# Half tiles of the expert stage: new load order, second side dealt from the far end, scatter-add in two parts

## The chip, the cores and the metric

The kernel runs on one core of one Trainium2 chip. The time is the device time of one launch in microseconds (us). Names used below: PE is TensorE, ACT is ScalarE, DVE is VectorE, POOL is GpSimd, SP is SyncE, whose only work here is to issue DMAs. PEclk is the granted TensorE clock, where 1.00 is 2.4 GHz and 0.50 is 1.2 GHz.

## The reference, cut to what matters

One decoder layer over 2048 prompt tokens and 64 sample tokens (D = 1024). The change touches only its last part, a mixture of experts: every token goes to 2 of 16 experts (both in the same group of four), each expert is a SwiGLU with weights of 1024 x 256 (gate), 1024 x 256 (up) and 256 x 1024 (down), all float32, and the two results are added per token:

```
eid = g_idx[:, None] * EXPERTS_PER_GROUP + top_i
hg = jnp.einsum('td,edf->tef', xt, w_gate)
hu = jnp.einsum('td,edf->tef', xt, w_up)
act = jax.nn.silu(hg) * hu * gates[..., None]
return jnp.einsum('tef,efd->td', act, w_down).reshape(shp)
```

After it comes a norm over each token's sum, a gain, and the addition of the residual x2.

## The kernel before

The expert stage (`moe`) sorts the 4224 pairs of token and expert by expert and cuts them into 42 tiles of 128 rows. The first 32 (`NWHOLE`) are whole: all rows belong to one expert, the weights are split in high and low parts, and a tile takes PE some 9.3 us. The last 10 (`NPAIR`, "steps" 0 to 9 below) hold the remainders: each has two halves, or sides, of 64 rows (`HROWS`), with an expert of its own. There is room for 20 halves (`NHALF`), numbered in the order of the experts; how many exist depends on the routing. Half h sits at step h on side 0 for h below 10, and at step h - 10 on side 1 otherwise. The pair of loads of a half that does not exist is issued with a condition that is false (`cond`, from `plan_h`), so it moves nothing.

For a step PE does, in this order: gate and up of tile t (`gate_up_halves`, L3150, 32 matmuls), the transpose of the tokens of tile t+2 (L3139), down of tile t-1 (`down_halves`, L3164, 16 matmuls), and the transpose of the activations (L3102). ACT copies the down result out of PSUM into one of two buffers `o` (L2732), and POOL adds it to the rows of `acc` in DRAM by an indirect DMA with addition (`store`, L2664). A token can occur in two tiles, so a store waits until the one before it has landed. ACT waits, before it fills a buffer of `o`, until the store two tiles back has landed. POOL's queue between two stores holds the routing weights of a later tile (`weigh`, L2653 to L2655) and the gather of the tokens of a later tile (`refill`, L2658).

SP issues the weight loads in program order: `half_gate_up` (L2564, two loads of 1 MB) and `half_down` (L2575, one of 1 MB). Rings of buffers: gate and up 5 deep on side 0 and 2 on side 1, down 3 and 2 (`GU_RING`, `D_RING`). A load waits until the tile that used its buffer is done; a wait of SP holds everything behind it. The order before is gate/up of (step, side) = (0,0), (0,1), (1,1), (1,0), (2,0), (3,0), (4,0), then down of (0,0), (0,1), (1,1), (1,0), (2,0), then per step the refills of the rings. In steps 5, 6, 7 and 8 SP also loads 5, 4, 4 and 4 tiles of the residual x2 (L2547, 0.5 MB each), behind that step's gate/up refill.

When all stores have landed, SP loads the 17 tiles of `acc` (L2620) and the other engines finish the output.

The slot of a pair is computed on DVE (L2906 to L2911, tiny instructions in a chain in which each waits for the one before), the row addresses of the scatter are `to` (L2941), one column for each tile.

Of the kernel before, what the change touches and what calls it, by code (L numbers as in the profile page):

```python
# [17 lines left out]
U32 = mybir.dt.uint32  # L18
ALU = mybir.AluOpType
# [3 lines left out]
P = 128  # L23
# [49 lines left out]
class Stage:  # L73
# [17 lines left out]
    def sem(self, name):  # L91
        return self.top.get(f"{self.tag}_{name}")
# [2267 lines left out]
HROWS = P // 2  # L2360
# [36 lines left out]
def moe(nc, T, top, lg, plan_in):  # L2397

    E16 = [P, NT, NE]
    with Stage(nc, top, "ex") as s:  # L2400
# [19 lines left out]
        et, plan = s.sb("et", [1, 4, NWHOLE]), s.sb("plan", [1, 3, NWHOLE], I32)  # L2420
        eh, plan_h = s.sb("eh", [1, 3, NHALF]), s.sb("plan_h", [1, 2, NHALF], I32)
# [38 lines left out]
        names = ("halved G2_in G2_samples eps_set warm tailed hit tiled tiled_late numbered tail_out weighed wt_ready to_ready summed rooted rstd gained gain_moved y_pool g_ready y_ready y_out cleared5 consts5 w5_in mm5 mod5 row5 out5 ident_in step de exped hot counted planned matched turned rows_ready x_flipped x_moved_a x_moved_v w_rounded w_split d_rounded d_split a_split gu_done th_ready "  # L2460
# [25 lines left out]
        yv = T["o_y_prompt"].rearrange("a (n p) d -> p (a n) d", p=P)  # L2486
        rows_of = lambda t: slice(0, NS) if t == LAST else slice(0, P)
# [11 lines left out]
        def _(sp):  # L2499
# [49 lines left out]
            def half_expert(step, side, always):  # L2549
                h = step + side * NPAIR  # L2550
                e = sp.value_load(plan_h[0:1, 0, h:h + 1], min_val=0, max_val=NE - 1)
                return e, {} if always else {"cond": sp.value_load(plan_h[0:1, 1, h:h + 1], min_val=0, max_val=1)}
# [40 lines left out]
            half_gate_up(2, 0)  # L2593
            half_gate_up(3, 0)
            half_gate_up(4, 0)
            half_down(0, 0)
            half_down(0, 1)
            half_down(1, 1)
            for step in range(NPAIR):
                if step == 0:  # L2600
                    half_down(1, 0)
                    half_down(2, 0)
                for side in (1, 0):
                    if step + GU_RING[side] < NPAIR:
# [20 lines left out]
            sp.wait_ge(S["st_even"], (HT + 1) * 16)  # L2625
            sp.wait_ge(S["st_odd"], (HT + 1) * 16)
# [8 lines left out]
        def _(pool):  # L2635
# [24 lines left out]
            def store(t):  # L2660
                pool.wait_ge(S["o_out_a"], t * 2 + 4)
                if t:
                    pool.wait_ge(sem("st", (t - 1) % 2), ((t - 1) // 2 + 2) * 16)
                pool.indirect_dma_start(T["acc"], bass.IndirectOffsetOnAxis(to[:, t:t + 1], 0), o[:, t % 2, :], None, compute_op=ALU.add).then_inc(sem("st", t % 2), 16)  # L2664
# [17 lines left out]
            pool.wait_ge(S["st_even"], (HT + 1) * 16)  # L2682
            pool.wait_ge(S["st_odd"], (HT + 1) * 16)
# [6 lines left out]
        def _(act):  # L2690
# [37 lines left out]
            def out(t, par, q):  # L2728
                act.wait_ge(S["d_done"], t + NSL + 1)
                act.wait_ge(sem("st", par), q * 16 + 16)  # L2730
                for c in range(2):
                    A(o[:, par, c * 512:(c + 1) * 512], ps_o[:, c * 512:(c + 1) * 512], ACT.Copy).then_inc(S["o_out_a"], 1)  # L2732
# [28 lines left out]
            def step(t, k, i, more=True):  # L2761
                par = k % 2
                gate(t, par)
                if more:
                    move_x(t + 2, par)
                    slot = weights_of(t + 2, (k + 2) % U, i + (k + 2) // U)
                    round_w(t + 2, par, range(PARTS // 2), slot)
                out(t - 1, 1 - par, i * (U // 2) + (k - 1) // 2)
# [15 lines left out]
            for t in range(NWHOLE - 2, NTILE):  # L2784
# [3 lines left out]
                out(t - 1, (t - 1) % 2, (t - 1) // 2)  # L2788
# [6 lines left out]
            out(NTILE - 1, 1, HT - 1)  # L2795
# [30 lines left out]
        def _(dve):  # L2826
# [425 lines left out]
```

## Time and profile before

| | us |
|---|---|
| median of 3 runs | 1485.31 (1484.14 to 1490.89) |
| profiled execution, its own time | 1483.67 |
| its span, first to last instruction | 1481.9 |
| last matmul of the last whole tile, to the last store landed | 1270.4 to 1432.7 |

Busy shares of the span: PE 87%, DVE 69%, ACT 48%, POOL 40%. All times in the rows are us from the start of the span. The page cuts the span into 40 equal slices of 37 us; a digit is the busy share in tenths. The stage of the half tiles lies in slices 35 to 39. In the rows of DMA queues, q1 carries the loads that SP issues, q0 those of POOL (gathers and scatter-adds); the share is that of the time of the core's 16 DMA engines, and the two together may come out a little over 1.

### The profile page before, as it was taken

The numbers are of one execution on the slowest core, as the hardware profiler recorded it, in microseconds if no ns is written. First come the engines' busy times: TensorE is split into PE (matmuls) and PEld (weight loads), VectorE is DVE, ScalarE is ACT, GpSimd is POOL, SyncE is SP. The second block draws the span as 40 slices with busy tenths as digits, with TensorE's granted clock in tenths as the row PEclk, the third lists the DMA queues.
The fourth block names the chain that finished last, engine by engine and source line by source line (L and its number), as shares of the span: only waits on it lengthen the run. The fifth ranks groups of instructions, "written<-read, shape, count | busy, mean of one in ns | idle before, by whom it ended". The sixth has DMA issues, their size and how long they took to land. (4 is left out here: it accounts for less than half of the span.)

```text
span 1481.9 us, 23003 instructions
## 1 busy us (share of the span) xinstructions
PE 1281.9 (87%) x6972; PEld 951.6 (64%) x6972; DVE 1017.3 (69%) x1914; ACT 708.9 (48%) x1551; POOL 596.2 (40%) x730
## 2 busy tenths in 40 slices
PE   4999999969998999699999996289999999669930
PEld 1688888846675666588888884178888888323310
DVE  3788888827676778566667764999999999200026
ACT  2432333213345768334444432268898998212234
POOL 1107766832223880022222330346565755212115
PEclk9999999979998999899999997599999999889975
DMA  9423444479897653335444446658999898999989
GB/s 328 147 88 128 164 168 179 167 232 335 297 298 181 188 175 121 127 110 166 161 145 142 142 138 231 220 173 228 299 314 278 245 281 239 315 337 342 330 254 365
DMA packets 163031, 325.30 MB, mean 220 GB/s; under 512 B 23140, under 2 KB 103141, under 8 KB 160590
## 3 DMA queue, kind: packets, MB, share of 16 engines
q1 hardware_dynamic: 136854, 251.88, 49.4%
q0 software_dynamic: 19072, 54.83, 14.8%
q10 hardware_dynamic: 7024, 17.60, 3.2%
q8 instruction: 40, 0.66, 0.2%
q14 instruction: 41, 0.34, 0.1%
HBM read 314.63 MB, written 97.73 MB: 278 GB/s over the span
## 5 line engine op out<-in xcount | busy, mean ns | idle before, releaser
L2664 POOL DMA_INDIRECT scratch_acc<-route_o,ex_to x42 | 80.6, 1918 | 235.1 <-ACT route_o L2732 138.1
L2929 DVE TENSOR_TENSOR ex_w_lo<-route_wgu,ex_w_hi 128x1024 fp32r<-128x1024 f32 x128 | 150.5, 1216 | 2.9 <-issue 1.9
L147 PE MATMUL fr_ps_m<-fr_whi,fr_hl 128*128 128x512 f32 (+1 forms) x384 | 138.8, 361 | 0.9 <-DVE fr_wlo L658 0.5
L149 PE MATMUL fr_ps_m<-fr_whi,fr_hl 128*128 128x512 f32 (+1 forms) x384 | 136.2, 355 | 0.0
L148 PE MATMUL fr_ps_m<-fr_wlo,fr_hl 128*128 128x512 f32 (+1 forms) x384 | 136.0, 354 | 0.0
L2035 POOL TENSOR_SCALAR mx_st<-mx_st 128x1 f32<-128x1 f32 x68 | 38.1, 561 | 228.9 <-ACT mx_j L2083 127.8
L2705 ACT ACTIVATE ex_w_hi<-route_wgu 128x1024 fp32r (+1 forms) x128 | 128.6, 1064 | 1.9 <-issue 1.9
L147 PE MATMUL mx_ps_m<-mw_area,mx_hT 128*128 128x512 f32 x272 | 108.8, 400 | 4.1 <-issue 2.1
L2999 DVE SCALAR_TENSOR_TENSOR ex_gates<-ex_gates,ex_ps_h 128x256 f32<-128x256 f32 x42 | 17.4, 414 | 133.6 <-ACT ex_gates L2713 133.2
L148 PE MATMUL mx_ps_m<-mw_area,mx_hT 128*128 128x512 f32 x272 | 107.2, 394 | 0.0
L149 PE MATMUL mx_ps_m<-mw_area,mx_h_lo 128*128 128x512 f32 x272 | 107.1, 394 | 0.0
L147 PE MATMUL ex_ps_h<-ex_w_hi,ex_xT 128*128 128x512 f32 x256 | 103.6, 405 | 0.1
L148 PE MATMUL ex_ps_h<-ex_w_lo,ex_xT 128*128 128x512 f32 x256 | 100.9, 394 | 0.0
L3150 PE MATMUL ex_ps_h<-route_wgu,ex_xT_whole 128*64 128x512 f32 x192 | 73.1, 622 | 14.2 <-DMA route_wgu<-in_w_exp_up_dram 14.2
L2653 POOL TENSOR_SCALAR ex_eq<-ex_x,route_rc 128x2 f32<-128x2 f32 x42 | 83.4, 1985 | 0.1
L147 PEld LDWEIGHTS fr_ps_m<-fr_whi,fr_hl 128*128 128x128 f32 x384 | 72.5, 189 | 15.0 <-issue 3.0
L451 ACT ACTIVATE fr_io<-fr_ps_m,fr_st 128x512 f32<-128x512 f32 (+1 forms) x45 | 27.4, 617 | 113.2 <-PE fr_ps_m L149 113.1
L148 PEld LDWEIGHTS fr_ps_m<-fr_wlo,fr_hl 128*128 128x128 f32 x384 | 72.6, 189 | 10.4
L149 PEld LDWEIGHTS fr_ps_m<-fr_whi,fr_hl 128*128 128x128 f32 x384 | 72.6, 189 | 10.3
L2969 DVE TENSOR_TENSOR ex_wd_lo<-route_wd,ex_wd_hi 128x1024 fp32r<-128x1024 f32 x64 | 76.2, 1231 | 3.2 <-ACT ex_wd_hi L2723 3.0
L1609 ACT ACTIVATE at_sc<-at_sc,at_nm 128x256 f32<-128x256 f32 (+1 forms) x128 | 62.7, 492 | 18.3 <-DVE at_nm L1689 18.2
L2732 ACT ACTIVATE route_o<-ex_ps_o 128x512 f32<-128x512 f32 x84 | 45.4, 595 | 47.1 <-PE ex_ps_o L3164 42.0
(544 smaller groups left out, 3562.0 us busy)
## 6 DMA issues: line engine op xcount, KB each, us to landing
route_wd<-in_w_exp_down_dram SPq DMA_DIRECT2D x46, 1024.0 KB, 10.0
route_wgu<-in_w_exp_gate_dram SPq DMA_DIRECT2D x44, 1024.0 KB, 12.8
route_wgu<-in_w_exp_up_dram SPq DMA_DIRECT2D x44, 1024.0 KB, 15.2
scratch_rec<-fr_w SPq DMA_DIRECT2D x16, 1112.0 KB, 4.2
s_rec<-scratch_rec SPq DMA_DIRECT2D x32, 556.0 KB, 6.3
scratch_proj<-fr_io SPq DMA_DIRECT2D x16, 640.0 KB
scratch_acc<-in_zeros_dram SPq DMA_DIRECT2D x18, 512.0 KB, 5.6
fr_w<-in_w_ada_dram SPq DMA_DIRECT2D x8, 1024.0 KB, 9.6
```

Of the source, the lines that this page charges most:

```text
L147: nc.tensor.matmul(out, hi, w_hi, start=first, stop=False)
L148: nc.tensor.matmul(out, hi, w_lo, start=False, stop=False)
L149: return nc.tensor.matmul(out, lo, w_hi, start=False, stop=final)
L1609: last = A(sc[:, p % 2, h, k0:], sc[:, p % 2, h, k0:], ACT.Exp, scale=-1.0, bias=nm[:, p % 2, h:h + 1], accum_out=sm[:, p % 2, h:h + 1])
L2035: last = nc.gpsimd.tensor_scalar(a[:, col + m:col + m + 1], a[:, col + m:col + m + 1], c, EPS, ALU.mult, ALU.add)
L2653: chain.then(nc.gpsimd.tensor_scalar(eq2[:, :], x[:, n, D + 2:], C["place"][:, t:t + 1], None, ALU.is_equal))
L2664: pool.indirect_dma_start(T["acc"], bass.IndirectOffsetOnAxis(to[:, t:t + 1], 0), o[:, t % 2, :], None, compute_op=ALU.add).then_inc(sem(" ...
L2705: A(w_hi[:, par, c * PW:(c + 1) * PW], wgu[:, bass.ds(slot * (KD * 2 * DE) + c * PW, PW)], ACT.Copy).then_inc(S["w_rounded"], 1)
L2732: A(o[:, par, c * 512:(c + 1) * 512], ps_o[:, c * 512:(c + 1) * 512], ACT.Copy).then_inc(S["o_out_a"], 1)
L2929: vec.tensor_tensor(w_lo[:, par, c * PW:(c + 1) * PW], wgu[:, bass.ds(slot * (KD * 2 * DE) + c * PW, PW)], w_hi[:, par, c * PW:(c + 1) * P ...
L2969: vec.tensor_tensor(wd_lo[:, k, :], wd[:, bass.ds(slot * (2 * D) + k * D, D)], wd_hi[:, k, :].bitcast(F32), ALU.subtract).then_inc(S["d_sp ...
L3150: last = nc.tensor.matmul(ps_h[rows, t % 2, :], xT_whole[t % 2][:, k, rows], gu_of(step, side)[:, k, :], start=(k == 0), stop=(k == KD - 1))
```

## The change

1. The half on side 1 of step s is now number 19 - s instead of 10 + s. On DVE this takes five small instructions where three were.
2. SP's order: the first down loads (0,0), (0,1), (1,1) come before gate/up (2,0); then down (1,0), gate/up (3,0), down (2,0), gate/up (4,0).
3. The store of each of the ten half tiles is two indirect DMAs of 64 rows, one per side. The second waits until the first has landed, and the next tile's store waits for the second. For the second, the addresses of rows 64 to 127 are copied to partitions 0 to 63 (`to_lower`), by one small DMA that POOL issues before its first store. All 64 rows of a side are transferred, whether the half exists or not (the addresses of rows without a token point behind the tokens' rows). `stored(t)` gives the value of the semaphore at which tile t has landed; the waits are rewritten with it.

```
@@ half_expert
-                h = step + side * NPAIR
+                h = NHALF - 1 - step if side else step
@@ sync
             half_gate_up(1, 1)
             half_gate_up(1, 0)
-            half_gate_up(2, 0)
-            half_gate_up(3, 0)
-            half_gate_up(4, 0)
             half_down(0, 0)
             half_down(0, 1)
             half_down(1, 1)
+            half_gate_up(2, 0)
             for step in range(NPAIR):
                 if step == 0:
                     half_down(1, 0)
+                    half_gate_up(3, 0)
                     half_down(2, 0)
+                    half_gate_up(4, 0)
@@ store
-                    pool.wait_ge(sem("st", (t - 1) % 2), ((t - 1) // 2 + 2) * 16)
-                pool.indirect_dma_start(T["acc"], bass.IndirectOffsetOnAxis(to[:, t:t + 1], 0), o[:, t % 2, :], None, compute_op=ALU.add).then_inc(sem("st", t % 2), 16)
+                    pool.wait_ge(sem("st", (t - 1) % 2), stored(t - 1))
+                if t < NWHOLE:
+                    pool.indirect_dma_start(T["acc"], bass.IndirectOffsetOnAxis(to[:, t:t + 1], 0), o[:, t % 2, :], None, compute_op=ALU.add).then_inc(sem("st", t % 2), 16)
+                    return
+                for side in range(2):
+                    h = slice(side * HROWS, (side + 1) * HROWS)
+                    if side:
+                        pool.wait_ge(S["lower_in"], 16)
+                        pool.wait_ge(sem("st", t % 2), stored(t) - 16)
+                    pool.indirect_dma_start(T["acc"], bass.IndirectOffsetOnAxis(to_lower[:, t - NWHOLE:t - NWHOLE + 1] if side else to[h, t:t + 1], 0), o[h, t % 2, :], None, compute_op=ALU.add).then_inc(sem("st", t % 2), 16)
@@ gpsimd
             pool.wait_ge(S["to_ready"], 1)
+            pool.dma_start(to_lower[:, :], to[HROWS:P, NWHOLE:]).then_inc(S["lower_in"], 16)
@@ vector
-            ts(side, half_no, NPAIR - 0.5, 1.0 - NHALF, ALU.is_ge, ALU.mult)
-            tt(half_no, half_no, side, ALU.add)
-            chain.then(vec.scalar_tensor_tensor(sf, half_no, float(HROWS), sf, ALU.mult, ALU.add))
+            ts(side, half_no, NPAIR - 0.5, None, ALU.is_ge, ALU.bypass)
+            chain.mark(vec.scalar_tensor_tensor(sf, half_no, float(HROWS), sf, ALU.mult, ALU.add))
+            ts(half_no, half_no, -4.0 * HROWS, (2.0 * NHALF - 1) * HROWS, ALU.mult, ALU.add)
+            tt(side, side, half_no, ALU.mult)
+            tt(sf, sf, side, ALU.add)
```

## Rows read from the trace of the kernel before

**Rows 1.** Page, the 40 slices: PE, DMA share, GB/s.
```profile
PE   4999999969998999699999996289999999669930
DMA  9423444479897653335444446658999898999989
GB/s 328 147 88 128 164 168 179 167 232 335 297 298 181 188 175 121 127 110 166 161 145 142 142 138 231 220 173 228 299 314 278 245 281 239 315 337 342 330 254 365
```
**Rows 2.** Waits, 1255 to 1435: who <- for whom: us in total, times, longest.
```profile
POOL scratch_acc L2664 <- DMA scratch_acc<-route_o,ex_to: 22.4, 4, 9.4
PE ex_ps_h L3150 <- DMA route_wgu<-in_w_exp_up_dram: 14.2, 1, 14.2
PE ex_ps_o L3164 <- DMA route_wd<-in_w_exp_down_dram: 11.9, 1, 11.9
```
**Rows 3.** Timeline of SP's DMA issues: start, us, what.
```profile
1259.52 0.64 SPq L2564 DMA_DIRECT2D route_wgu<-in_w_exp_gate_dram  x1
...
1262.34 1.56 SPq L2564 DMA_DIRECT2D route_wgu<-in_w_exp_gate_dram  x1
1264.00 7.39 SPq L2564 DMA_DIRECT2D route_wgu<-in_w_exp_up_dram  x1
1272.83 0.17 SPq L2564 DMA_DIRECT2D route_wgu<-in_w_exp_gate_dram  x1
...
1301.39 7.62 SPq L2575 DMA_DIRECT2D route_wd<-in_w_exp_down_dram  x3
```
**Rows 4.** Timeline: DVE's last split of down weights, PE's first gate/up of halves.
```profile
1272.66 2.36 DVE L2969 TENSOR_TENSOR ex_wd_lo<-route_wd,ex_wd_hi 128x1024 fp32r<-128x1024 f32 x2 [0.62 <-ACT ex_wd_hi L2723]
...
1284.60 9.38 PE L3150 MATMUL ex_ps_h<-route_wgu,ex_xT_whole 128*64 128x512 f32 x32 [14.20 <-DMA route_wgu<-in_w_exp_up_dram]
```
**Rows 5.** The chain that ended last, in order of time: start, us, what.
```profile
1318.08 6.27 PE ex_ps_o L3164 x16
...
1324.71 7.02 PE ex_ps_h L3150 x32
1331.73 1.08 PE ex_ps_t L3139 x8
1332.82 3.58 PE ex_ps_o L3164 x16
...
1407.91 7.02 PE ex_ps_h L3150 x32
1414.92 3.46 PE ex_ps_o L3164 x16
1418.40 1.09 ACT route_o L2732 x2
...
1419.82 6.29 DMA scratch_acc<-route_o,ex_to
1426.15 0.50 issue
1426.86 5.80 DMA scratch_acc<-route_o,ex_to
```
**Rows 6.** DMA view, 1262 to 1416: queue, packets, MB, share of 16 engines.
```profile
q1 hardware_dynamic: 28098, 43.02, 80.3%
q0 software_dynamic: 2491, 9.10, 24.0%
```
**Rows 7.** Stretches: us, busy of PE, PEld, DVE, ACT, POOL, PEclk, DMA share, GB/s.
```profile
1295.00:1300.00 5.00, 5.00 (x25) 3.03 (x25) 0.37 (x1) 2.45 (x5) 0.76 (x1) 1.00 1.10 350
...
1310.00:1315.00 5.00, 0.00 (x0) 0.00 (x0) 0.00 (x0) 0.00 (x0) 0.00 (x0) 0.50 1.05 410
...
1415.00:1420.00 5.00, 3.91 (x20) 1.25 (x18) 0.90 (x2) 1.72 (x4) 0.18 (x1) 1.00 0.64 151
```
**Rows 8.** Timeline of POOL: two stores in a row [idle before <- releaser].
```profile
1398.18 1.58 POOL L2664 DMA_INDIRECT scratch_acc<-route_o,ex_to  x1 [9.47 <-ACT route_o L2732]
...
1410.09 1.59 POOL L2664 DMA_INDIRECT scratch_acc<-route_o,ex_to  x1 [9.43 <-DMA scratch_acc<-route_o,ex_to]
```
**Rows 9.** DMA view, 1426.9 to 1432.7: engines' busy tenths in 40 slices.
```profile
DMA  0000000000000099037696959599999999820000
```
**Rows 10.** Timeline: DVE's slot arithmetic, then POOL's issue of a small DMA.
```profile
943.88 0.19 DVE L2830 TENSOR_TENSOR ex_stau<-ex_stau,ex_srow 128x34 f32<-128x34 f32 x1
944.11 0.22 DVE L2911 SCALAR_TENSOR_TENSOR ex_tail<-ex_stau,ex_tail 128x34 f32<-128x34 f32 x1
...
927.87 0.53 POOL L2643 DMA_DIRECT2D ex_row<-in_b_ada_dram  x1 [0.29 <-POOL ex_row L2639]
```

More of the change, by code:

```diff
@@ L2420, in moe @@
         et, plan = s.sb("et", [1, 4, NWHOLE]), s.sb("plan", [1, 3, NWHOLE], I32)
+        to_lower = s.sb("to_lower", [HROWS, NPAIR], U32)
         eh, plan_h = s.sb("eh", [1, 3, NHALF]), s.sb("plan_h", [1, 2, NHALF], I32)
@@ L2459, in moe @@
         junk = wd[:, 3 * D:4 * D]
-        names = ("halved G2_in G2_samples eps_set warm tailed hit tiled tiled_late numbered tail_out weighed wt_ready to_ready summed rooted rstd gained gain_moved y_pool g_ready y_ready y_out cleared5 consts5 w5_in mm5 mod5 row5 out5 ident_in step de exped hot counted planned matched turned rows_ready x_flipped x_moved_a x_moved_v w_rounded w_split d_rounded d_split a_split gu_done th_ready "
+        names = ("lower_in halved G2_in G2_samples eps_set warm tailed hit tiled tiled_late numbered tail_out weighed wt_ready to_ready summed rooted rstd gained gain_moved y_pool g_ready y_ready y_out cleared5 consts5 w5_in mm5 mod5 row5 out5 ident_in step de exped hot counted planned matched turned rows_ready x_flipped x_moved_a x_moved_v w_rounded w_split d_rounded d_split a_split gu_done th_ready "
                  "sg_ready a_ready a_flipped a_moved d_done o_out_a st_even st_odd").split()
@@ L2486, in moe @@
         yv = T["o_y_prompt"].rearrange("a (n p) d -> p (a n) d", p=P)
+        stored = lambda t: (t // 2 + 2 + max(0, (t - NWHOLE) // 2 + 1)) * 16
         rows_of = lambda t: slice(0, NS) if t == LAST else slice(0, P)
@@ L2624, in _ @@
             sp.dma_start(G2[:, 0, :], mod_row(T, 5)).then_inc(S["G2_in"], 16)
-            sp.wait_ge(S["st_even"], (HT + 1) * 16)
-            sp.wait_ge(S["st_odd"], (HT + 1) * 16)
+            sp.wait_ge(S["st_even"], stored(NTILE - 2))
+            sp.wait_ge(S["st_odd"], stored(NTILE - 1))
             for t in range(NT):
@@ L2681, in _ @@
                 store(t)
-            pool.wait_ge(S["st_even"], (HT + 1) * 16)
-            pool.wait_ge(S["st_odd"], (HT + 1) * 16)
+            pool.wait_ge(S["st_even"], stored(NTILE - 2))
+            pool.wait_ge(S["st_odd"], stored(NTILE - 1))
             for n, t in enumerate(BY_POOL):
@@ L2726, in slot_of, with out @@
                 return act.value_load(plan[0:1, 2, bass.ds(t, 1)], min_val=0, max_val=NSL - 1)
-            def out(t, par, q):
+            def out(t, par, landed):
                 act.wait_ge(S["d_done"], t + NSL + 1)
-                act.wait_ge(sem("st", par), q * 16 + 16)
+                act.wait_ge(sem("st", par), landed)
                 for c in range(2):
@@ L2767, in step @@
                     round_w(t + 2, par, range(PARTS // 2), slot)
-                out(t - 1, 1 - par, i * (U // 2) + (k - 1) // 2)
+                out(t - 1, 1 - par, (i * (U // 2) + (k - 1) // 2) * 16 + 16)
                 move_a(t)
@@ L2787, in _ @@
                     move_x_whole(t + 2)
-                out(t - 1, (t - 1) % 2, (t - 1) // 2)
+                out(t - 1, (t - 1) % 2, stored(t - 3))
                 if t < NWHOLE:
@@ L2794, in _ @@
                     A(aT[:, :, :], ps_a[:, 0:2 * P].rearrange("p (k n) -> p k n", k=2), ACT.Copy, scale=0.5).then_inc(S["a_moved"], 1)
-            out(NTILE - 1, 1, HT - 1)
+            out(NTILE - 1, 1, stored(NTILE - 3))
             act.wait_ge(S["eps_set"], 1)
```

## Prediction

> **What bounds the kernel now.** The slices of the page come first: PE is near full almost everywhere, and in the stage of the half tiles (slices 35 to 38) it drops while the DMA share stands at 9 [rows 1]. The waits of that stretch name what PE waits for: once 14.2 us for the gate/up weights of step 0, once 11.9 us for the down weights of step 0 [rows 2]. SP's timeline tells why. Gate/up (0,0) is issued at 1259.52, (0,1) at 1262.34, and then come 6 MB of gate/up for steps 2 to 4 before the first down load at 1301.39 [rows 3]. The same timeline tells how many halves exist: a load that moves data takes SP 0.6 us or far more once the queue is full, one whose condition is false 0.17 us. (0,1) is real, (1,1) at 1272.83 is not, nor is any later load of side 1. So there are 11 halves: ten on side 0, one on side 1. The bytes agree: 11 halves of 3.15 MB and 16.5 tiles of x2 of 0.524 MB are 43.3 MB, and q1 moved 43.02 MB from 1262 to 1416 [rows 6].
>
> The same rows hold what decides. Over those 154 us the two queues take 80.3% + 24.0%, more than all of the DMA engines' time. They are full from the first half's load until the last x2 tile, and only after 1415 does the share fall (0.64) [rows 6, 7]. PE's two stalls are thus a matter of order, but the stretch as a whole is also bound by DMA. From step 1 on, PE runs at 7.02 + 1.08 + 3.58 + 0.37 = 12.06 us a step [rows 5]. At the end, two stores follow each other: from 1419.82 to 1432.7 [rows 5].
>
> **The change part by part.**
>
> *The first steps.* Half number 19 doesn't exist, so (0,1) moves nothing, and gate/up (0,0) alone has to land before step 0. In the trace both together, 4.2 MB, let PE start at 1284.6 [rows 4]; without 2.1 MB, at the 350 GB/s of gate/up loads [rows 7], that is 6 us earlier. Two of q0's DMAs then also fall behind the data instead of ahead of it; q0's 2491 packets are 17 DMAs of 144, 24.0% of 154 us is 37 us, so 2.1 us each [rows 6]. That gives 1284.6 - 6 - 4.2 = 1274.4. PE could start at 1284.6 - 14.2 = 1270.4, so the stall becomes some 4 us. Down (0,0) can be issued from 1275.0, when DVE has split the last whole tile [rows 4], and lands long before PE wants it at about 1293: the 11.9 us go. With them goes the slow clock: 9.38 us for 7.02 at step 0 and 6.27 for 3.58 at the first down, both right after PE had stood idle and the granted clock was 0.50 [rows 4, 5, 7]. From step 0's gate/up to its down the trace has 1318.08 - 1284.60 = 33.5 us, without the 11.9 and the cold clock's 2.4 it is 19.2, so PE reaches the down of step 0 at 1293.6 instead of 1318.1, and runs it warm: 27 us are gained at this point. If DMA could follow, this would be the gain.
>
> *The moved half.* Half number 10 now sits at step 9, side 1: the 2.1 MB of gate/up (9,1) and the 1.05 MB of down (9,1). SP issues them in step 7, behind the x2 tiles of steps 5 and 6 and the down loads of steps 7 to 9. No byte is taken away, so the full stretch is as long as before, and (9,1) stands near its end. Behind gate/up (9,1) come only the x2 tiles of steps 7 and 8 (7.5 x 0.524 = 3.9 MB) and down (9,1) (1.05 MB): 5 MB, which at the 410 GB/s of loads with rows of 4 KB [rows 7] take 12.1 us. Gate/up (9,1) lands at 1416 - 12.1 = 1404, with half a microsecond for the signal 1404.5. PE, free for step 2's gate/up at 1297.5 and at 12.06 us a step, would want it at about 1381, so it stalls for some 23 us: the stall of the start has moved to the end. Step 9 starts 3.4 us before its time in the trace (1407.91) [rows 5], and a cold clock takes 2.4 us of it back. From there the path is the old one: 1.0 us gained. Bounds: 1401 if the queue wastes nothing, 1406 if the new order leaves gaps in the queue (down (1,0) makes SP wait for the last whole tile). I find none, because gate/up (1,0) and (2,0) are still queued then.
>
> *The order of loads* alone costs nothing beyond that: each load is still ahead of its use while the rings fill (gate/up (3,0) and (4,0) closest, about 1 us).
>
> *The split store, idle DMA.* The last two stores of 128 rows take 6.29 and 5.80 us with 0.50 and some more between them [rows 5]. In the last one, 14 of the 40 slices of 0.145 us pass before the first packet and 22 with packets: 2.1 us, 3.2 us, and 0.5 us for the rest [rows 9]. 64 rows halve the middle: 2.1 + 1.6 + 0.5 = 4.2 us, and with the issue between two DMAs 4.9. If the issue (1.58 us) halves too it is 4.1; the trace has no such store. Bounds for one: 2.9 and 5.8. I take 4.5. Four in a row make 18.0 us where two took 12.9: 5.1 us later.
>
> *The split store, full DMA.* The store at 1398.18 held the next one up until 1410.09: 11.9 us [rows 8], against 6.5 with the engines idle, so 5.4 us more under load. A half bears between half of that (2.7, if it grows with the rows) and all of it. This gives 7.2 to 9.9 us a half, 14.4 to 19.8 a pair. I take 7.75 and 15.5, nearer to the lower end because the rows queue behind the loads one by one. That is more than PE's 12.06, so POOL falls behind by 3.4 us a step. ACT's wait for the buffer two tiles back hides this for six or seven steps, and `weigh` and the gather, which stand behind the second half on POOL, are wanted two tiles later. First store of a half tile at 1298 (1293.6 + 3.6 + 1.1 of ACT); that of step 7 starts at 1298 + 7 x 15.5 = 1406.5 and ends, its second half with the queue easing, at 1420.3. Step 8's result leaves ACT at 1404.5 + 9.4 + 3.5 + 1.1 = 1418.5, so the lag adds 1.8 us. Then 18.0: the last store lands at 1438.3, against 1432.7: 5.6 us later. The stretch after it keeps its 49 us.
>
> *Small things.* Two more chained DVE instructions of 0.19 to 0.22 us [rows 10], on the way to the first gather: 0.4 us. The copy of `to_lower`: 0.5 us on POOL's queue [rows 10], ahead of `weigh`, which PE isn't waiting for: 0.1. Together 0.5.
>
> Sum: 5.6 + 0.5 = 6.1 us. The profiled execution of 1483.67 (span 1481.9 and 1.8 around it) becomes 1489.8; the median lies 1.6 above that execution, so 1485.3 + 6.1 = **1491.4**.
>
> The Trainium skill (DMA: Bandwidth & Descriptors, the section on the anatomy of a SWDGE DMA) gives 2.0 us plus bytes at 436 GB/s for one of POOL's DMAs. By it a store of 128 rows is an estimated 3.2 us and one of 64 rows 2.6, so that a pair costs 2 us more at any load and the tail 4. The trace has 5.8 to 11.9 us for 128 rows, so the page's figure is low for a DMA that adds; what it says for this change is that the fixed part is most of it, which speaks for the forecast at the end and against POOL falling behind.
>
> **The rivals.**
>
> *A, the halves are cheap:* a store costs in proportion to its rows, 2.9 us and 0.7 between them, loaded 6. Then a pair takes 12 us under load, POOL keeps up, and the tail is 4 x 3.6 = 14.4 for 12.9. 1.5 + 0.5 - 1.0 = +1.0: 1486.3. Against it: a third of the store at the end passes before its first packet [rows 9].
>
> *B, POOL's chain becomes the bound (slower):* each half carries all of the load's 5.4 us, 19.8 us a pair. POOL is behind by 7.7 us a step, from step 4 on ACT waits for its buffer and PE for ACT. The load eases only at about 1416, after six steps (1298 + 6 x 19.8), and the last four pairs take 9 each: 1453, 20 us late: 1505.8. It decides from 16.5 us a pair on. For it: the wait before the first packet is a fixed part.
>
> *C, DMA has room (faster):* the share above 1 contains waiting, and with loads in the order of use the engines finish the same bytes sooner. Then (9,1) lands near 1385, the stall is some 7 us, PE ends 20 us early, and the pairs are those of an idle queue: 4.5 x 2 a step, never behind. -19 + 5.1 + 0.5 = -13: 1472. Against it: the 43 MB and the stores filled 154 us without a gap [rows 6], and loads ran at the same 350 and 410 GB/s when PE stood [rows 7].
>
> *D, the deal does not do what it says:* if half 19 were loaded at step 0 the first stall would stay and only the down stall go. Eleven halves by two counts make this unlikely; it would give about 1495.
>
> **How the numbers follow.** Forecast (2 to 10 us late) 0.53, A 0.13, B 0.19, C 0.13, D 0.02. About 0.5%, 7.4 us, is what a measurement of this kernel can tell from no change. Slower by more: all of B and D and the upper 0.2 of the forecast, 0.41. Faster by more: most of C, 0.12. Within: 0.47. Range: from A's lower side, with C left out, 1480, to short of B's end, 1504.
>
> **What would show it.** In the changed profile PE's waits should read a few us for gate/up at step 0, none for down, and one of 20 us or more for gate/up at step 9; the DMA share from 1262 to about 1415 stays at 1; q1 carries the same 43 MB. Stores of 64 rows under load start 7 to 8 us apart and 4 to 5 at the end, and the last lands near 1438. If PE does not stall at step 9, the ledger of DMA time is wrong; if PE or ACT wait for stores before step 8, it is B.

## The result, and the profile after

| | before | after |
|---|---|---|
| median | 1485.31 us | 1510.85 us (1506.99 to 1512.86, 3 runs) |
| ratio | | 1.0165, 95% interval 1.0142 to 1.0188 |
| profiled execution | 1483.67 | 1512.86 |
| its span | 1481.9 | 1511.1 |
| first gather of the stage | 956.07 | 962.60 |
| PE free for half tiles | 1270.40 | 1281.38 |
| last store landed | 1432.7 | 1461.1 |

The change makes the kernel 25.5 us slower. 6.1 were forecast, and the range ended at 1504: the prediction named the right direction, was wrong in size and missed its range.

The two spans differ by 29.2 us. The last three rows of the table cut that up. 6.5 lie ahead of the first gather; 0.35 of them are the two more DVE instructions, and the rest is in code that is the same in both kernels. Over all builds below, this point falls anywhere between 954.5 and 962.8, and the kernel before by itself took 1480.2 to 1493.1 us in 17 runs on one chip, so it is put down to chance here. 4.5 lie between the first gather and PE free for half tiles (314.3 before, 318.8 after). 17.4 lie in the stage of the half tiles, counted from PE free to the last store landed (162.3 before, 179.7 after), and 0.8 behind it. Below, "the stage" is that last-but-one stretch; it doesn't contain the chance shift of the first one. Of these the forecast had 0.4 of the first and 5.6 of the third; it had nothing for the second.

The page after, the same lines as [rows 1]:

```profile
PE   5999999969998999799999993499999999799700
...
DMA  9424444489897562344444438649999898999759
```

PE's hole in slices 35 and 36 (6 and 6 before) is half filled, with 7 and 9. A new one stands in slices 38 and 39 (7 and 0 for 9 and 3), where the DMA share falls to 7 and 5: neither is the bound there. The waits of 1255 to 1465, as [rows 2], say more (columns: who <- for whom: us in total, times, longest):

```profile
POOL scratch_acc L2674 <- DMA scratch_acc<-route_o,ex_to: 56.4, 9, 8.1
ACT route_o L2743 <- DMA scratch_acc<-route_o,ex_to_lower: 40.6, 5, 12.1
...
DVE ex_gates L3015 <- POOL ex_wt L2657: 17.9, 4, 6.9
POOL scratch_acc L2674 <- DMA scratch_acc<-route_o,ex_to_lower: 17.8, 4, 5.5
...
PE ex_ps_h L3163 <- DMA route_wgu<-in_w_exp_up_dram: 8.1, 1, 8.1
...
PE ex_ps_h L3163 <- issue: 4.1, 1, 4.1
```

The 14.2 and 11.9 of PE are gone, as forecast; 4.1 is what is left at step 0 (forecast: 4). But PE waits 8.1 us once more for gate/up, not at step 9 but at step 2, and ACT, which waited for no store before, waits 40.6 us for second parts (`ex_to_lower`).

What PE waits for at step 2 is in SP's timeline (start, us, what):

```profile
1272.85 0.17 SPq L2566 DMA_DIRECT2D route_wgu<-in_w_exp_gate_dram  x1
...
1300.14 5.93 SPq L2566 DMA_DIRECT2D ex_spare<-in_w_exp_up_dram  x1
1306.83 3.89 SPq L2577 DMA_DIRECT2D ex_wd_spare<-in_w_exp_down_dram  x1
1311.50 0.55 SPq L2566 DMA_DIRECT2D ex_spare<-in_w_exp_gate_dram  x1
1312.15 4.42 SPq L2566 DMA_DIRECT2D ex_spare<-in_w_exp_up_dram  x1
1317.98 0.18 SPq L2566 DMA_DIRECT2D route_wgu<-in_w_exp_gate_dram  x1
1318.26 0.16 SPq L2566 DMA_DIRECT2D route_wgu<-in_w_exp_up_dram  x1
```

The first row is (0,1): 0.17 us, so it moves nothing, and the deal does what it says. The last two are gate/up (2,1), a half that doesn't exist either. They move nothing, yet PE waits for their signal, and SP reaches them only after gate/up (3,0), down (2,0) and gate/up (4,0), each of which holds SP for 4 to 6 us while the DMA share is 1.0 or more (an issue of 1 MB takes 0.6 us when DMA has room). PE's timeline:

```profile
1306.40 3.65 PE L3177 MATMUL ex_ps_o<-route_wd,ex_aT 128*64 128x512 f32 x16
...
1318.53 1.09 PE L3163 MATMUL ex_ps_h<-ex_spare,ex_xT_whole 128*64 128x512 f32 x1 [8.11 <-DMA route_wgu<-in_w_exp_up_dram]
```

PE starts 0.11 us after SP is through with (2,1). The chain that ended last, as [rows 5], goes through this point and is then almost nothing but stores:

```profile
1318.53 9.33 PE ex_ps_h L3163 x32
1327.86 1.09 PE ex_ps_t L3152 x8
1328.95 3.61 PE ex_ps_o L3177 x16
1332.58 1.09 ACT route_o L2743 x2
1333.68 0.27 issue
1333.95 7.28 DMA scratch_acc<-route_o,ex_to
1341.26 0.71 issue
1341.97 7.63 DMA scratch_acc<-route_o,ex_to_lower
1349.65 0.71 issue
1350.36 7.47 DMA scratch_acc<-route_o,ex_to
...
1429.13 4.62 DMA scratch_acc<-route_o,ex_to
1433.80 0.71 issue
1434.51 4.42 DMA scratch_acc<-route_o,ex_to_lower
...
1456.46 4.65 DMA scratch_acc<-route_o,ex_to_lower
```

The gate/up matmuls of step 2 take 9.33 us and not 7.02: behind PE's wait the granted clock is 0.50 until 1323 ("cold clock" below), then 0.99. From 1333.95 on each part waits for the one before. Before, the same stretch was PE's 12.06 us a step [rows 5]; now it is POOL's pairs.

### The profile page after: what moved, and what is told of

Same layout as the page of the kernel before. It is cut to its first block and busy times, and to the rows that moved or that the text cites. A ratio compares the mean times of both kernels' runs of the same rounds, so it can differ in the third digit from the quotient of the medians.

```text
span 1511.1 us, 23025 instructions
## 1 busy us (share of the span) xinstructions
PE 1294.3 (86%) x6972; PEld 954.4 (63%) x6972; DVE 1017.9 (67%) x1916; ACT 709.4 (47%) x1551; POOL 620.5 (41%) x741
## 5 line engine op out<-in xcount | busy, mean ns | idle before, releaser
L149 PE MATMUL fr_ps_m<-fr_whi,fr_hl 128*128 128x512 f32 (+1 forms) x384 | 136.0, 354 | 0.0
L2667 POOL DMA_INDIRECT scratch_acc<-route_o,ex_to x32 | 59.8, 1870 | 119.9 <-ACT route_o L2743 58.9
L149 PE MATMUL mx_ps_m<-mw_area,mx_h_lo 128*128 128x512 f32 x272 | 107.3, 394 | 0.0
L3012 DVE SCALAR_TENSOR_TENSOR ex_gates<-ex_gates,ex_ps_h 128x256 f32<-128x256 f32 x42 | 17.4, 415 | 114.9 <-ACT ex_gates L2724 114.9
L147 PEld LDWEIGHTS fr_ps_m<-fr_whi,fr_hl 128*128 128x128 f32 x384 | 72.5, 189 | 14.2 <-issue 3.3
L3163 PE MATMUL ex_ps_h<-route_wgu,ex_xT_whole 128*64 128x512 f32 x192 | 76.8, 639 | 4.1 <-issue 4.1
L149 PEld LDWEIGHTS fr_ps_m<-fr_whi,fr_hl 128*128 128x128 f32 x384 | 72.5, 189 | 10.3
L2743 ACT ACTIVATE route_o<-ex_ps_o 128x512 f32<-128x512 f32 x84 | 45.5, 596 | 58.3 <-DMA scratch_acc<-route_o,ex_to_lower 40.6
## 6 DMA issues: line engine op xcount, KB each, us to landing
route_wgu<-in_w_exp_gate_dram SPq DMA_DIRECT2D x44, 1024.0 KB, 12.9
```

The costliest lines, as they stand in the source:

```text
L147: nc.tensor.matmul(out, hi, w_hi, start=first, stop=False)
L149: return nc.tensor.matmul(out, lo, w_hi, start=False, stop=final)
L3163: last = nc.tensor.matmul(ps_h[rows, t % 2, :], xT_whole[t % 2][:, k, rows], gu_of(step, side)[:, k, :], start=(k == 0), stop=(k == KD - 1))
```

## The experiments

Each kernel's time is given with its ratio to the kernel before on the same chip (1485.3 to 1488.1 us in the four sets of runs) and its 95% interval, then its whole-tile part and its stage.

| kernel | us | ratio | whole tiles | stage |
|---|---|---|---|---|
| before | 1485.31 | | 314.3 | 162.3 |
| after | 1510.85 | 1.0165 (1.0142, 1.0188) | 318.8 | 179.7 |
| e1_order | 1479.34 | 0.9953 (0.9927, 0.9980) | 313.9 | 159.7 |
| e2_split | 1520.32 | 1.0243 (1.0216, 1.0270) | 318.8 | 193.6 |
| e4_one_side | 1482.08 | 0.9986 (0.9967, 1.0005) | 318.8 | 155.4 |
| e5_ahead | 1504.46 | 1.0153 (1.0109, 1.0197) | 318.8 | 177.2 |
| g_no_wait | 1490.57 | 1.0029 (1.0009, 1.0050) | 318.8 | 164.9 |
| f1_order_ahead | 1483.80 | 0.9975 (0.9955, 0.9996) | 315.9 | 158.5 |
| f3_one_ahead | 1482.46 | 0.9967 (0.9945, 0.9989) | 318.8 | 155.2 |
| f4_one_ahead_x2 | 1487.79 | 1.0004 (0.9979, 1.0028) | 318.8 | 160.4 |
| p1_room | 1490.26 | 1.0026 (1.0003, 1.0049) | 318.7 | 161.1 |
| p2_after64 | 1507.97 | 1.0143 (1.0098, 1.0189) | 318.8 | 180.4 |
| e3_last_split | 1488.54 | 1.0022 (1.0000, 1.0045) | 318.8 | 161.7 |
| c1_rot | 1481.25 | 0.9983 (0.9955, 1.0012) | 314.0 | 158.7 |
| q1_room_last | 1503.72 | 1.0116 (1.0094, 1.0138) | 314.3 | 181.6 |
| d2_last_split_room | 1486.78 | 1.0010 (0.9991, 1.0028) | 315.0 | 162.1 |

**The order of loads alone.** The kernel before with the new order:

```
-            half_gate_up(2, 0)
-            half_gate_up(3, 0)
-            half_gate_up(4, 0)
             half_down(0, 0)
             half_down(0, 1)
             half_down(1, 1)
+            half_gate_up(2, 0)
...
                     half_down(1, 0)
+                    half_gate_up(3, 0)
                     half_down(2, 0)
+                    half_gate_up(4, 0)
```

> The kernel before with the new load order alone; half number 10 stays at step 0, stores stay whole. The profile of the changed kernel shows a stall that the prediction had not seen: gate/up of step 2 waited 8.1 us for the load (2,1), which moves nothing and is issued last, behind gate/up (3,0) and (4,0), while SP was held by the full DMA queue. Theory Q (place in SP's queue): the 11.9 us wait for down of step 0 goes, a wait for (2,1) of some us comes; PE is 5 to 12 us ahead at step 2. The DMA engines are full until about 1416 all the same, but behind the last weights stand only x2 tiles, so 3 to 7 us of it last: 1479 to 1483. Theory D (DMA bound, order worth nothing): 1485.

The runs say 0.5% faster, the profile 2.6 us less in the stage. The 11.9 us for down weights are gone, but PE's waits for gate/up now read

```profile
PE ex_ps_h L3150 <- DMA route_wgu<-in_w_exp_up_dram: 23.7, 2, 13.9
```

13.9 at step 0 as before, and 9.8 at step 2, for (2,1): its two empty DMAs are issued at 1322.24 and 1322.51, and PE starts at 1322.78. The order saves 11.9 us and the 2.7 of cold clock at the first down; the wait at step 2 and its cold clock (8.95 us for 7.02) take back 9.8 and 1.9, which leaves 2.9. The trace shows just that: PE is free for half tiles at 1273.29 and not at 1270.40, and from 1336.77 on every matmul group of the chain stands at the same time as in the kernel before, up to step 9's gate/up at 1407.91 [rows 5]. So the wait at step 2 belongs to the order of loads, not to deal or split, and it takes back most of what the order gains.

**The split alone.** The changed kernel with the order of loads and the deal put back (DVE's slot arithmetic too):

```
-                h = NHALF - 1 - step if side else step
+                h = step + side * NPAIR
...
```

> The kernel before with the stores of the half tiles in two parts alone; order and deal as before. Theory P (POOL's chain of stores is the bound): pairs of 16 us while the loads run, 10.7 after. First pair at 1326, six pairs to about 1420, four more to 1463, which is 30 us behind the kernel before: 1515. PE's two stalls at step 0 stay. If the split only costs at the end (the forecast's tail alone): 4 x 5.2 for 12.9, +8 us, 1493. If the loss of the changed kernel came from the order of loads (theory Q alone), this one is at 1489 or less.

1520.3, 5.3 above the 1515 given for theory P; 4.5 of them are in the whole tiles (318.8, see the place of to_lower below).

```profile
POOL scratch_acc L2674 <- DMA scratch_acc<-route_o,ex_to: 52.9, 9, 7.7
...
ACT route_o L2743 <- DMA scratch_acc<-route_o,ex_to_lower: 40.0, 5, 12.2
...
PE ex_ps_h L3161 <- DMA route_wgu<-in_w_exp_up_dram: 13.8, 1, 13.8
PE ex_ps_o L3175 <- DMA route_wd<-in_w_exp_down_dram: 12.1, 1, 12.1
```

The stage grows by 31.3 us: this is the loss, and ACT's wait (40.0 in 5) is that of the changed kernel (40.6 in 5). Both stalls of PE are there too, and they hide none of it, since they lie ahead of the first pair. That pair starts 54.7 us after PE is free, about where the first store of a half tile started before (55.4). Seven pairs then take 104.7 us for 84.3, and from step 7's store to the end it is 34.2 us for 22.6.

**The same without the wait between the parts.**

```
                     if side:
                         pool.wait_ge(S["lower_in"], 16)
-                        pool.wait_ge(sem("st", t % 2), stored(t) - 16)
```

> The kernel before with the stores of the half tiles in two parts (as in the run with the split alone, 1520.3), but the second part is issued at once, without waiting for the first to land. With the deal of before, the two halves of a tile never hold the same token, so nothing is lost. Theory W (what costs is that the parts wait for each other): a pair lands like one whole store plus 1.4 us of issue, 12 to 13 us under load and 8 at the end; POOL keeps up nearly, 1487 to 1492. Theory S (two small DMAs cost the engines more than one large): pairs stay at 15 us or more and the time above 1505.

The stage falls from 193.6 to 164.9. POOL's timeline, with the start, us and the idle time before it:

```profile
1366.58 1.45 POOL L2673 DMA_INDIRECT scratch_acc<-route_o,ex_to  x1 [6.79 <-ACT route_o L2742]
1368.33 1.43 POOL L2673 DMA_INDIRECT scratch_acc<-route_o,ex_to_lower  x1 [0.30 <-issue]
...
1378.82 1.47 POOL L2673 DMA_INDIRECT scratch_acc<-route_o,ex_to  x1 [8.17 <-ACT route_o L2742]
```

The parts are issued 1.75 us apart and each pair 12 us after the last: PE sets the pace again, and the same 128 rows move in the same two DMAs. What costs is that the second waits for the first to land. 28.7 of the split's 31.3 us are this.

**The first part only.** The changed kernel, with one part in steps 0 to 8 (it leaves the second part out; its rows hold nothing here):

```
-                for side in range(2):
+                for side in range(2 if t == NTILE - 1 else 1):
...
```

> The changed kernel, with the second part of the store left out for steps 0 to 8. The halves of side 1 of these steps do not exist, so the addresses of these rows point behind the tokens' rows, and nothing of the output is left out. Step 9 keeps both parts. Theory P: a store takes 8 us under load, less than PE's 12.06 us a step, so POOL never falls behind, ACT waits for no store, and what is left is the ledger of DMA time: gate/up (9,1) lands near the time that the forecast gave, PE stalls there, and the end is 0 to 4 us behind the kernel before: 1485 to 1490. Theory Q (the 10 us lost at step 2 are the cause): they stay, 1495 to 1500.

1482.1, 2.9 us below the range given, so on theory P's side. 155.4 us of stage against 179.7 gives the second parts 24.3 us, their bytes and their waits together. PE waits at step 2 (8.6) and at step 9 (3.3). A stall at step 9 was forecast for the changed kernel, but one of 23 us; there it doesn't appear at all, because ACT and PE are late by then through the stores.

**Asking for (2,1) ahead of (3,0).** Three kernels, the changed one, the one with the order alone, and the one with the first part only, get

```
                     half_down(1, 0)
+                    half_gate_up(2, 1)
                     half_gate_up(3, 0)
...
-                    if step + GU_RING[side] < NPAIR:
+                    if step + GU_RING[side] < NPAIR and (step, side) != (0, 1):
```

> The changed kernel, with one load moved in SP's order: gate/up (2,1), which moves nothing, directly behind down (1,0) instead of behind gate/up (4,0). Theory Q: the wait of 8.1 us at step 2 goes with its cold clock of 2.3; step 2 starts near 1311 instead of 1318.5 (times of the changed profile). Theory P: the chain of stores is the bound from then on, so it starts 10 us earlier and ends 8 to 10 us earlier: 1501 to 1503. If the chain were bound by something else (DMA), the time stays at 1511.

> The kernel before with the new order alone (1479.3) and gate/up (2,1), which moves nothing, ahead of (3,0). There PE waited 9.8 us for (2,1) at step 2. Theory Q: the wait goes, step 2's gate/up starts at 1311 to 1314 instead of 1322.8, nothing later is late, and the end moves with it: 1470 to 1474. Theory D (DMA bound): down weights of the last steps, which stand behind the x2 tiles, come late, and less than half of it is kept: 1475 to 1479.

> The changed kernel with the second part left out for steps 0 to 8 (its rows hold nothing, as before) and with gate/up (2,1) ahead of (3,0). The stalls of 8.6 us at step 2 and of some 10 us at step 9 were left in the run without the second part (1482). Theory D (the ledger of DMA time sets when gate/up (9,1) lands, whatever PE did before): PE gains 8 to 10 us at step 2, waits as much longer at step 9, and the time stays: 1480 to 1483. Theory P' (PE's own path set the end): 1472.

The wait at step 2 goes in all three, and the next absent load takes its place: PE waits 6.7, 6.2 and 7.8 us at step 3, for (3,1). The stage is 2.5 us shorter in the changed kernel, 1.2 with the order alone and 0.2 with the first part only. All three expectations failed, in the time or in its reason. With the order alone the time is 10 us above the range given. The changed kernel took 1504.5 for the 1501 to 1503 given, but of the 8.8 us between the two profiled executions 6.2 are the chance shift of the first stretch; 8 to 10 were expected of the stage. With the first part only the time came out as given (1482.5), but PE didn't wait longer at step 9, as theory D had it (3.4 us, 3.3 before): the new wait at step 3 took the gain. One empty request moved isn't a cure: the next one, (3,1), stood behind gate/up (5,0), which held SP for 6 to 10 us.

The first of the three tells one thing more. Step 1's pair starts 46.13 us after PE is free and not 52.57. Of these 6.4 us 4.1 are left at step 7's pair and 2.5 at the end, since the pairs are slower: 16.3 us each from step 1 to step 7 for 15.9, at a DMA share of 1.02 for 0.99, and 33.6 us from step 7's store to the end for 32.0.

**The x2 tiles later.** The third of them, with x2 asked for behind the last down weights:

```
-                if step == 5:
-                    load_x2_past(5, range(0, 5))
...
+                if step == 7:
+                    load_x2_past(7, range(0, 13))
```

> As the run before it, and the x2 tiles of steps 5 to 7 are loaded after the last down weights instead of ahead of gate/up (9,1). 9 tiles of 0.524 MB, 11.5 us at 410 GB/s, no longer stand before it. Theory D: gate/up (9,1) lands 8 to 11.5 us sooner, the stall at step 9 shrinks by that, and the x2 tiles fit beside the last steps and stores: 1470 to 1474. If the x2 tiles were not what held it, or if they now end after the last store, 1480 or more.

1487.8: a miss, and the other case that was named (this kernel leaves the second parts out too). If gate/up (9,1) were late by the bytes ahead of it, it would come early here. Two stretches (busy of PE, PEld, DVE, ACT, POOL, then PEclk, DMA share, GB/s), then SP's issue of down (8,1) and (9,0) and of gate/up (9,1), then PE's start of step 9:

```profile
1370.00:1380.00 10.00, 10.00 (x48) 3.33 (x48) 0.48 (x1) 2.45 (x5) 2.21 (x4) 1.00 0.32 88
1380.00:1390.00 10.00, 10.00 (x50) 3.72 (x48) 0.90 (x2) 2.83 (x6) 2.19 (x4) 1.00 0.26 66
```

```profile
1386.11 1.93 SPq L2577 DMA_DIRECT2D route_wd<-in_w_exp_down_dram  x2
1389.47 0.62 SPq L2566 DMA_DIRECT2D route_wgu<-in_w_exp_gate_dram  x1
1390.18 0.84 SPq L2566 DMA_DIRECT2D route_wgu<-in_w_exp_up_dram  x1
```

```profile
1400.39 1.08 PE L3160 MATMUL ex_ps_h<-ex_spare,ex_xT_whole 128*64 128x512 f32 x1 [3.40 <-DMA route_wgu<-in_w_exp_up_dram]
```

For 20 us DMA is mostly idle, and still (9,1) is issued at 1389.47. By the code it needs the buffer of (7,1), since side 1's ring has two places. PE is through with step 7's gate/up at 1381.1, but SP doesn't get to (9,1) for 8.3 us more: down (8,1), an absent half, stands before it and waits for a buffer that PE frees with the down of step 6, at 1385.8. So the same thing holds SP here as at step 2, its place in the program order behind an empty request, now with a wait and not a full queue. (9,1) lands 10 us after its issue, and PE waits 3.4 us for it; asked for when its buffer was free, and as long under way, it would not have been late (an estimate, no run shows it). The x2 tiles then meet the stores of step 8 and of step 9's first side, which take 7.9 and 6.9 us.

**Order and deal with whole stores.** The changed kernel, whole stores in steps 0 to 8, the last tile in two parts:

```
-                if t < NWHOLE:
+                if t < NTILE - 1:
...
```

> The changed kernel with order and deal as they are, but the results of steps 0 to 8 stored as whole tiles of 128 rows, as in the kernel before; only the last tile is stored in two parts. Nothing of the computation is left out. Theory W (what the change loses is the wait between the two parts of each step, 15.9 us a pair): a whole tile's store is 11 to 12 us loaded, under PE's 12 us a step, so the stage is that of the run with the second part left out, 155 to 157 us, and the time 1482 to 1486. Rival (order and deal together lose on their own, through the wait at step 2 and the load of step 9): 1490 or more.

1488.5, 2.5 us above the range given, and below the rival's 1490. The stage of 161.7 is 18.0 less than with every tile split, but 155 to 157 were expected. The forecast of the moved half can be read here, since the stores no longer hide it. PE waits 7.1 us at step 9; the 13.7 of the chain are the whole of the load, from its issue on:

```profile
1390.89 0.62 SPq L2566
1391.60 13.70 DMA route_wgu<-in_w_exp_up_dram
1405.43 8.78 PE ex_ps_h L3163 x32
```

**The place of to_lower.** All kernels with that tile spend 318.8 us in the whole tiles, in unchanged code, and those without it 313.9 to 315.9. The kernel before with one line more, and nothing that uses it:

```
+        to_lower = s.sb("to_lower", [HROWS, NPAIR], U32)
         eh, plan_h = ...
```

> The kernel before with one line more: the tile to_lower (64 rows of ten numbers) is given its place in the core's memory at the same point as in the change, and nothing uses it. Every kernel with that tile spends 4.5 us more between the first gather of the stage and the end of the whole tiles, in code that is the same. Theory L (the place: all tiles that are given theirs later lie 40 bytes further on, and the matmuls of the whole tiles are slower by it): 318.8 us from the first gather to PE free for half tiles in place of 314.3, and the time is 4 to 5 us over the kernel before (1489 to 1493). Rival (it is the added transfer, the added semaphore or the two instructions more of DVE): 314.3 as before, and the time within 0.2% of it.

318.7 us, and 1490.3. The groups of PE of 1000 to 1240, in this kernel (first two rows) and in the one that follows in this section with the tile last (the other two); after the colon busy us and mean ns:

```profile
L147 PE MATMUL ex_ps_h<-ex_w_hi,ex_xT 128*128 128x512 f32 x203 | 82.4, 406 | 0.0
L148 PE MATMUL ex_ps_h<-ex_w_lo,ex_xT 128*128 128x512 f32 x204 | 80.6, 395 | 0.0
```

```profile
L147 PE MATMUL ex_ps_h<-ex_w_hi,ex_xT 128*128 128x512 f32 x204 | 81.8, 401 | 0.1
L148 PE MATMUL ex_ps_h<-ex_w_lo,ex_xT 128*128 128x512 f32 x204 | 79.6, 390 | 0.0
```

5 ns a matmul, at a granted clock of 1.00 in both. Of the other five groups of this stretch three are 4 to 6 ns slower as well; the two that read `x_lo_even` and `a_lo` differ by 1 ns and by nothing. Over the counts of the groups this adds up to some 4.8 us for the whole tiles (an estimate), which fits the 4.5. Then the changed kernel with the tile 16 columns wide, and with the tile allocated last:

> The changed kernel with to_lower given 16 columns in place of ten (64 bytes a row; the six more are not used), so that the tiles behind it lie 64 bytes further on than before and not 40. Theory L, in the form that it is the odd 40 bytes: the whole tiles take 314.3 us again, and the time is 1505 to 1507. L in another form (any shift): 318.8 us and 1510.9, as the change. Rival (the added transfer, the semaphore or DVE's instructions): 318.8 and 1510.9 too; the other kernel of this call, which has the place alone, tells these two apart.

> The changed kernel with to_lower given its place last of all tiles, so that every other tile lies where it did in the kernel before; nothing else differs. Theory L (the place of the other tiles makes the matmuls of the whole tiles slower): 314.3 us from the first gather to PE free for half tiles, the stage of half tiles as in the change (179 us), and 4 to 5 us less in all: 1505 to 1508. Rival (the added transfer or the instructions of the change bring the 4.5 us as well, beside the place): 318.8 and 1510.

64 bytes more are no better than 40 (318.8). With all other tiles back in their place it is 314.3, in the full changed kernel. So the 4.5 us are the place of the tiles, and the added transfer, semaphore and instructions cost nothing there. The median of 1503.7 is 1.3 below the range given. It is 7.1 below 1510.85, though the stage is 1.9 longer in its profile; 4.5 of it is explained, the rest is of the size by which the first stretch varies. Which tile must lie where, and why, wasn't tried: the slower matmuls include some that read only tiles ahead of `to_lower` (L149 with `x_lo_odd`, 397 for 392 ns).

> Order, deal and the last tile in two parts, whole stores in steps 0 to 8, with to_lower given its place last of all tiles. The same kernel with to_lower where the change has it took 1488.5 and waited 13.7 us at step 9 for the load of the moved half. Theory L: 4 to 5 us less, 1483 to 1485, so that order, deal and the split last tile together are worth no more than the order of loads alone (1479.3, and the moved half's wait at step 9 is why). Rival (the wait at step 9 is one of DMA bytes that fall later against an earlier PE, and grows by what PE gains): the same 1488.

1486.8, 2 above the range, and the profile's 315.0 and 162.1 carry L. PE waits 9.6 at step 2 and 6.4 at step 9. Order and deal together, with the last tile in two parts, leave the stage where it was before (162.3).

**Half 10 at step 1.**

```
-                h = step + side * NPAIR
+                h = NPAIR + (step - 1) % NPAIR if side else step
...
```

> The kernel before with the new order of loads, whole stores, and the second side dealt with a turn by one: the one half of that side that holds rows comes at step 1 in place of step 0 (the last, empty one at step 0). Two sizes of the same mechanism: if the first three steps are bound by the bytes (the same bytes are wanted by step 1), PE only waits at step 1 in place of step 0, and the time is that of the new order alone, 1478 to 1481. If they are bound by PE behind its first load (step 0 starts 10 us earlier and its work is done before step 1's load is there), 4 to 9 us less: 1470 to 1475. The wait at step 2 for the absent load stays in both.

1481.3: the upper case. PE waits 5.5 at step 0 instead of 13.9, then 2.9 at step 1, and 12.5 at step 2 instead of 9.8, so that the start only moves its wait; the stage is 1.0 shorter than with the order alone.

No kernel here has a lower median than the order of loads alone, 1479.34 us; the intervals of f1_order_ahead, f3_one_ahead and c1_rot overlap with its own.

## Why the prediction was wrong, point by point

**What was right.** The down stall goes and step 0's gate/up wait shrinks to 4.1 (4 forecast). The two parts at full DMA (share 0.99) take 15.9 us a pair, six of them from 1333.95 to 1429.13 in 95.2 us (15.5 forecast). q1 carries the same bytes (DMA view, 1262 to 1420; [rows 6] ends at 1416):

```profile
q1 hardware_dynamic: 28156, 42.95, 76.9%
q0 software_dynamic: 2694, 9.46, 24.8%
```

**What came out near by luck.** The moved half, without the stores' help: in the run with order, deal, last split and `to_lower` last it lands 130.0 us after PE is free (1400.9 - 1270.9), forecast 134.1 (1404.5 - 1270.4). But PE wanted it at 123.8 us and not at 110.6: 9.6 of wait at step 2, 1.7 of cold clock there and 1.8 at step 0 were not in the forecast. So the stall of 23 us was one of 6.4. The stage is 0.2 us shorter than before; the forecast's own terms give 1.6 longer for this kernel (1.0 gained, and 6.5 + 2 x 4.5 for 12.9 at the end). The sum held to 2 us, with two errors in it that cancel. So did the 31.8 us from the start of step 7's store to the end (32.0): step 7's pair took 10.5 us for 13.8, the last four parts 21.4 for 18.0.

**The step that failed: "The order of loads alone costs nothing beyond that: each load is still ahead of its use".** That counted the loads that move data. An absent half's load is ahead of nothing by itself: it waits its turn on SP, and SP stands 4 to 6 us in each load of a full queue. [rows 3] had both sides of it, the 7.39 us of one gate/up load and the 0.17 of an empty one. The wait is 8.1 us, and 2.3 of cold clock come with it. Of this the second store's start shows 7.0: step 1's pair starts 22.5 us after step 0's (1311.46 to 1333.95) and not 15.5, because POOL then waits for PE. How much of the 7.0 reaches the end is another matter: without the wait for (2,1), but with the one for (3,1), the stage was 2.5 us shorter.

**The step that failed second, and cost more: that the lag of the pairs is hidden but for 1.8 us.** The mechanism was named in the forecast, and in rival B, with the sign that ACT waits for stores before step 8. It does, from step 5's result on (at 1382.76, behind an idle time of 4.5 us for step 3's second part). The forecast hid the lag in PE's stall at step 9: step 8's result 148.1 us after PE is free (1418.5), the pairs at 149.9 (1420.3). Measured, step 8's pair starts at 158.3 (1439.67), and with whole stores up to there (order, deal, last split, `to_lower` last) ACT has step 8's result ready at 143.9. So the lag is 14.4 us: the 1.8, 8.4 more because the pairs come later, and 4.2 because step 9's load, and with it step 8's result, comes earlier than the stall of the forecast allowed. With the 3.4 of the last four parts that is the 18 us that splitting steps 0 to 8 costs between the runs.

By the forecast's own numbers the pairs already decided, by 1.8 us, so what makes them later shows in the time:

| | us late against the forecast |
|---|---|
| first pair starts 30.1 us after PE is free, 27.6 forecast (1.8 of it: gate/up of step 0 cold, 8.78 for 7.02) | 2.5 |
| step 1's pair, PE late by (2,1) | 7.0 |
| six pairs of 15.86 and not 15.5 | 2.2 |
| from step 7's store to the end (3.3 less and 3.4 more) | 0.2 |

That is 11.9; with the 5.6 forecast it gives the 17.4 of the stage to 0.1. It is a ledger of this one trace, not a price list: a pair that starts earlier meets more loads, as the run with (2,1) asked for ahead showed (6.4 us gained at step 1, 2.5 at the end). The split alone points the same way: its first pair starts 24.6 us later than in the changed kernel and its stage is 13.9 longer, with a pair every 14.95 us at a DMA share of 0.92. That the pace follows the load is thus seen in three runs and not tested by itself.

B was the right case, with 19.8 us a pair where 15.9 were measured, and it had the wrong bound. Where "it decides from 16.5 us a pair on" comes from is not said; by the forecast's sum (1298 + 7 pairs + 13.8 against 1418.5) the bound is 15.2, below the 15.5 taken. The 11.9 us of [rows 8], from which the pairs were priced, run from start to start, for one of the two slowest stores of the stage: in that trace 128 rows land 8.9 to 11.2 us after the issue.

**`weigh` behind the second part.** It was said to be wanted two tiles later. DVE waited 17.9 us for it in four waits, and PE 9.7 for DVE, by the waits. But by then the pairs were the chain, so it stands in no term above.

**The idle parts** were put at 4.5 us each; the last four start 5.2 to 6.2 apart and land in 4.4 to 4.7. Two of them:

```profile
1439.67 1.42 POOL L2674 DMA_INDIRECT scratch_acc<-route_o,ex_to  x1 [3.75 <-DMA scratch_acc<-route_o,ex_to_lower]
...
1456.46 1.40 POOL L2674 DMA_INDIRECT scratch_acc<-route_o,ex_to_lower  x1 [4.02 <-DMA scratch_acc<-route_o,ex_to]
```

The Trainium skill (DMA: Bandwidth & Descriptors, the section on the anatomy of a SWDGE DMA) would give 2.6 us for one, an estimate from its 2.0 us and 436 GB/s. The measurement is 4.65. That the fixed part is most of it agrees: from 128 to 64 rows the DMA falls only from 5.80 [rows 5] to 4.65, so that by these two some 3.5 us don't depend on the rows, and the issue falls from 1.58 to 1.41 us.

**The place of the tiles** was in no term: 4.5 us. The "small things" had 0.5 for instructions and nothing for a tile in the middle of the others.

**The ledger of DMA time** gave a landing of (9,1) that was 4 us late, but not for its reason. With DMA idle (share 0.32 and 0.26, x2 put off) the load came no earlier: SP got to it 8.3 us after its buffer was free. Rival C, that DMA has room, didn't come: from 1262 to 1420 the two queues took 76.9% + 24.8%, as the forecast had it, and PE was never 20 us early.

In all, of the 29.2 us between the two profiled executions 17.4 (the parts that wait for each other) and 4.5 (the place of the tiles, whose own reason is open) have a cause that a run above shows, and 0.35 more are the two instructions. The medians are 25.5 apart; the 3.7 between the two figures are of the size by which the first stretch varies.

## What to carry to other kernels

Before a transfer is split into parts that wait for each other, add up the chain of the parts from its first link and compare it with the pace of the engine that feeds it. If the two are near, a delay ahead of the chain shows at the end, in part at least, and a stall that is only forecast is no cover. When loads are reordered, follow what waits for each request, the empty ones too: a request that moves nothing still stands behind whatever blocks its queue. And allocate a new small tile last, or measure its place alone.

## What the runs showed of the hardware

- A tile that nothing uses, allocated ahead of others, makes most of the 128x512 matmuls of the whole tiles some 5 ns slower each (401 to 406, 390 to 395 ns), 4.5 us in all, with the clock granted in full. This was seen in every kernel with the tile ahead of the others, and in neither of the two with it last (314.3 and 315.0). Its cause is open.
- A scatter-add of 64 rows of 4 KB takes, in the changed kernel, 4.4 to 4.7 us with DMA idle and 7.1 to 8.9 loaded (once 5.3); one of 128 takes 5.8 to 6.6 idle and, in the kernel before, 8.9 to 11.2 loaded. Pairs of 64 rows that wait for each other took 14.95, 15.9 and 16.3 us at DMA shares of 0.92, 0.99 and 1.02. Two of 64 rows that don't wait for each other took 6.8 us together (1434.03 to 1440.85).
- An indirect DMA occupies POOL's queue for 1.4 us at 64 rows and 1.6 at 128.
- The conditional load that moves nothing takes 0.15 to 0.19 us of SP, but signals only when SP gets there: PE started 0.11 us after it. A load of 1 MB takes SP 0.6 us, or up to 7.4 us at a DMA share of 1.
